# Memory keys and values computed under the second normalisation and kept in DRAM, two barriers taken out, and a gate product placed between the steps of the memory attention

## The reference, cut to what matters

```python
x = first_block(...)                          # ends with  h + y @ w_out   (w_out0, w_out1)
h = rmsnorm(x, g_mix)                         # "norm h2"
gq, gk, gv, gg, ga, dq, dk, dv, iq, ik, iw, mq, gates = split(h @ w_in)
o_gla = gla(gq, gk, gv, gg, ga)               # 4 linear-attention heads, state carried over 8 chunks
o_dsa = dsa(dq, dk, dv, iq, ik, iw)           # 8 heads; 128 keys chosen for each query by top-k
mem_h = rmsnorm(mem, g_mem)                   # 256 memory rows of 1024: does not depend on x
k, v = split(mem_h @ w_mem_kv)                # [256, 2048]; keys normalised for each of 4 heads
o_mem = softmax(norm(mq) @ norm(k).T) @ v     # 4 heads of 256
merged = sum(sigmoid(gates[b] + bias[b]) * (o_b @ w_o_b) for b in (gla, dsa, mem))
x = x + merged @ w_out                        # then 16 experts, 2 for each token
```

## Time and profile before

| | us |
|---|---|
| median of 3 runs (1584.70 to 1585.95) | 1585.25 |
| profiled execution, its own time | 1584.4 |
| its span, first to last instruction | 1582.5 |
| PE busy | 1393.1 (88% of the span) |
| DVE / ACT / POOL busy | 582.9 / 532.2 / 415.4 |
| mean granted TensorE clock | 0.923 of full |

### The profile page before, as it was taken

How to read it: one execution, slowest core, us unless ns; L and a number is a source line. 1 busy time by engine, 2 the same in 40 slices (tenths; PEclk the granted TensorE clock), 3 DMA queues, 4 the chain that set the end, 5 groups by cost and what they waited for, 6 DMA issues and landing times. The chain is left out here.

```text
span 1582.5 us, 16443 instructions
## 1 busy us (share of the span) xinstructions
PE 1393.1 (88%) x6220; PEld 1030.6 (65%) x6220; DVE 582.9 (37%) x1322; ACT 532.2 (34%) x945; POOL 415.4 (26%) x201
## 2 busy tenths in 40 slices
PE   4999979997789998999888976999799998699992
PEld 3777756675667766758667865877678876344440
DVE  2195554424221142349954433131341234221213
ACT  4442323213234463543335453244342224010100
POOL 3265211001233322215222213475205431000001
PEclk9999989857999999999989997999799998699996
DMA  4232423002222312113121213244105433799815
GB/s 139 61 92 67 154 67 101 22 2 70 80 67 66 95 33 74 54 53 107 60 65 49 61 53 99 94 142 125 45 17 197 173 120 147 305 358 366 298 67 187
DMA packets 75015, 175.35 MB, mean 111 GB/s; under 512 B 11166, under 2 KB 21588, under 8 KB 68788
## 3 DMA queue, kind: packets, MB, share of 16 engines
q1 hardware_dynamic: 67312, 161.28, 30.5%
q0 software_dynamic: 2592, 8.41, 1.5%
q10 hardware_dynamic: 5028, 4.55, 1.1%
HBM read 151.15 MB, written 23.07 MB: 110 GB/s over the span
## 5 line engine op out<-in xcount | busy, mean ns | idle before, releaser
L792 POOL TENSOR_TENSOR w_lo<-raw,w_hi 128x1024 fp32r<-128x1024 f32 (+1 forms) x158 | 377.6, 2407 | 884.4 <-ACT w_hi L1499 884.3
L887 PE MATMUL ps<-w_hi,act_hi 128*128 128x512 f32 (+1 forms) x560 | 236.0, 421 | 5.5 <-ACT dq L1659 4.0
L888 PE MATMUL ps<-w_lo,act_hi 128*128 128x512 f32 (+1 forms) x560 | 221.7, 396 | 0.0
L1499 ACT ACTIVATE w_hi<-raw 128x1024 fp32r<-128x1024 f32 (+1 forms) x158 | 158.7, 1033 | 186.5 <-PE ps L889 185.1
L889 PE MATMUL ps<-w_hi,act_lo 128*128 128x512 f32 (+1 forms) x560 | 220.9, 395 | 0.0
L887 PE MATMUL ps<-w_hi,mix_hi 128*128 128x512 f32 x320 | 134.1, 419 | 17.5 <-DVE gate L2157 9.9
L887 PEld LDWEIGHTS ps<-w_hi,act_hi 128*128 128x128 f32 (+1 forms) x560 | 106.1, 189 | 47.1 <-issue 15.2
L889 PE MATMUL ps<-w_hi,mix_lo 128*128 128x512 f32 x320 | 128.1, 400 | 0.0
L888 PE MATMUL ps<-w_lo,mix_hi 128*128 128x512 f32 x320 | 128.0, 400 | 0.0
L888 PEld LDWEIGHTS ps<-w_lo,act_hi 128*128 128x128 f32 (+1 forms) x560 | 106.1, 189 | 25.6 <-issue 3.3
L889 PEld LDWEIGHTS ps<-w_hi,act_lo 128*128 128x128 f32 (+1 forms) x560 | 105.6, 189 | 25.6
(11 more groups left out here) (419 smaller groups left out, 2027.1 us busy)
## 6 DMA issues: line engine op xcount, KB each, us to landing
raw<-in_w_in SPq DMA_DIRECT2D x92, 512.0 KB, 3.6
gu<-in_w_gate SPq DMA_DIRECT2D x16, 1024.0 KB, 6.5
gu<-in_w_up SPq DMA_DIRECT2D x16, 1024.0 KB, 8.7
dn<-in_w_down SPq DMA_DIRECT2D x16, 1024.0 KB, 9.9
x_rows<-zeros SPq DMA_DIRECT2D x16, 512.0 KB, 4.9
raw<-in_w_out SPq DMA_DIRECT2D x16, 512.0 KB, 4.0
raw<-in_w_mem_kv SPq DMA_DIRECT2D x16, 512.0 KB, 3.9
xe<-x_rows SPq DMA_DIRECT2D x16, 512.0 KB, 9.3
```

Source lines behind the costliest of these rows:

```text
L792: pool.tensor_tensor(lo[:, 0:a], raw[:, g % RAW_SLOTS, 0:a], hi[:, 0:a].bitcast(F32), ALU.subtract).then_inc(*POOL.done(("w_lo", g)))
L887: pe.matmul(dst, l_hi, r_hi, start=start, stop=False, skip_group_check=skip)
L888: pe.matmul(dst, l_hi, r_lo, start=False, stop=False, skip_group_check=skip)
L1499: nc.scalar.activation(split_slot(g)[0][:, 0:a], raw[:, g % RAW_SLOTS, 0:a], ACTF.Copy).then_inc(*ACT.done(("w_hi", g)))
```

## The change

The memory norm and its products move to the end of the first block and around `norm("h2")`; keys and values are written to two DRAM tensors and read back before the memory attention; the barriers `mem` and `mem2` go; `w_o00` joins the list that the top rounds are spread over; 12 parts of `gate20` and four query transposes go between the memory attention steps; three takes no longer stand ahead of the first block's attention; the turn of linear heads 1 and 3 moves ahead of the values of the head before.

```diff
@@ mla_order
     fill += [tail[0:2], tail[2:4]]
-    order, fill = sum(fill[0:3], []), fill[3:]
-    order += [("mla_transposes", 0), ("mla_transposes", 1)]
+    order = [("mla_transposes", 0), ("mla_transposes", 1)]
...
-    return order
+    last = item("w_out1")
+    return order + [("norm_scale", "mem")] + last[0:8] + [("norm", "mem")] + last[8:]
@@ make_order
-    order += mla_order() + item("w_out1") + [("barrier", "gla")]
-    order += [("norm", "h2")] + item("small2", "gla_q", "gla_k")
+    order += mla_order() + item("mem_kv0") + [("barrier", "gla"), ("norm_scale", "h2")] + item("mem_kv1") + [("mem_scale", "k")]
+    order += item("mem_kv2") + [("norm", "h2"), ("mem_prepare", "k")] + item("mem_kv3")
+    order += item("small2", "gla_q", "gla_k")
...
-    for h in range(GLA_H):
-        order += [("gla_states", h), ("gla_values", h)]
-        if h == 1:
-            order += [("gla_decays", 2)] + g0[0:8] + [("gla_decays", 3), ("gla_rstd", 0)] + g0[8:]
+    order += [("gla_turn", 0), ("gla_update", 0), ("gla_turn", 1), ("gla_values", 0), ("gla_update", 1), ("gla_values", 1)]
+    order += [("gla_decays", 2)] + g0[0:8] + [("gla_decays", 3), ("gla_rstd", 0)] + g0[8:]
+    order += [("gla_turn", 2), ("gla_update", 2), ("gla_turn", 3), ("gla_values", 2), ("gla_update", 3), ("gla_values", 3)]
...
-    dense += [("dsa_prepare", "q0"), ("dsa_scale", "q1")] + item("gate00") + [("dsa_prepare", "q1")]
-    order += spread(dense, rounds) + item("w_o00")
+    dense += [("dsa_prepare", "q0"), ("dsa_scale", "q1")] + item("gate00") + [("dsa_prepare", "q1")] + item("w_o00")
+    order += spread(dense, rounds)
...
-    order += [("mix_dsa",), ("barrier", "mem"), ("norm_scale", "mem"), ("norm", "mem")]
-    order += item("w_o10", "gate11", "w_o11", "mem_kv0", "mem_kv1") + [("mem_scale", "k")]
-    order += item("mem_kv2", "mem_kv3", "mem_q0")
-    order += [("mem_prepare", "k"), ("mem_scale", "q0")] + item("mem_q1") + [("mem_prepare", "q0"), ("mem_scale", "q1")]
-    order += [("mem_prepare", "q1"), ("barrier", "mem2")]
+    order += [("mix_dsa",)] + item("w_o10", "gate11", "w_o11", "mem_q0") + [("mem_scale", "q0")]
+    order += item("mem_q1") + [("mem_prepare", "q0"), ("mem_scale", "q1")]
     n = NT * MEM_H
+    steps = []
     for j in range(n + 3):
-        order += [("mem_values", j - 3)] * (j >= 3) + [("mem_turn", j - 2)] * (2 <= j < n + 2) + [("mem_scores", j)] * (j < n)
-    order += item("gate20", "w_o20", "gate21", "w_o21")
+        steps += [[("mem_values", j - 3)] * (j >= 3) + [("mem_turn", j - 2)] * (2 <= j < n + 2) + [("mem_scores", j)] * (j < n)
+                  + [("mem_turn_q", j + 2)] * (2 <= j < 6)]
+    g2 = item("gate20")
+    order += [x for s in spread(steps, [[p] for p in g2 if p[3] < 3]) for x in s] + [p for p in g2 if p[3] == 3]
+    order += [("route_start",)] + item("w_o20", "gate21", "w_o21")
@@ program
-        MEM_BANKS = (7, 3, 1, 2, 7, 3, 1, 2)
+        MEM_BANKS = (7, 3) * 4
+        def split_upto(name, u, b):
+            if name == "gate20":
+                ends = {0: min(u + 3, KC // 2), NT - 1: u + 4}
+            else:
+                ends = {0: u + 3}
+            return min(len(units), first_unit[name] + ends[b]) if b in ends else None
@@ sync
+                    if names[g] == ("gla_v0", 0):
+                        sp.wait_ge(*ACT.after("mkT", KC - 1))
+                        sp.dma_start(mem_keys, mkT_new[:, :, :].rearrange("p c n -> p (c n)")).then_inc(mem_spilled, 16)
+                        sp.wait_ge(*ACT.after("mkv", 3, 1))
+                        sp.dma_start(mem_vals, mv_new[:, :, :].rearrange("p c n -> p (c n)")).then_inc(mem_spilled, 16)
+                    if names[g] == ("mem_q0", 0):
+                        sp.wait_ge(mem_spilled, 32)
+                        sp.wait_ge(*PE.after("d_O", NT * DSA_H - 1))
+                        sp.wait_ge(*DVE.after("mix_lo", "dsa", DSA_H - 1))
+                        sp.dma_start(mkT[:, :, :].rearrange("p c n -> p (c n)"), mem_keys).then_inc(mem_back, 16)
+                        sp.dma_start(mv[:, :, :].rearrange("p c n -> p (c n)"), mem_vals).then_inc(mem_back, 16)
@@ scalar, norm_scale
                 if name == "mem":
+                    for h in (MLA_H - 2, MLA_H - 1):
+                        act.wait_ge(*PE.after("qT", "mla", h))
+                        act.wait_ge(*PE.after("kT", "mla", h))
+                    for t in range(2):
+                        act.dma_start(mem_in[:, t, :], w["mem_2"][0, P * t:P * t + P, :]).then_inc(mem_landed, 16)
                     act.wait_ge(mem_landed, 32)
@@ tensor, new step; scores
+            def mem_turn_q(c):
+                claim(6, (ACT, ("mqT", c)))
+                for t in range(NT):
+                    pe.wait_ge(*DVE.after("mqn", 1, t))
+                    tr = pe.transpose(ps[:, 6, P * t:P * t + P], mq[:, t, P * c:P * c + P], ident[:, :])
+                tr.then_inc(*PE.done(("mqT", c)))
             def mem_scores(j):
+                if j == 0:
+                    pe.wait_ge(mem_back, 32)
+                pe.wait_ge(*ACT.after("mqT", 2 * h + 1))
@@ scalar and vector: the seven routing DMAs of barrier mem2 and DVE's r_start are now the step route_start
+            def route_start():
+                act.wait_ge(*PE.after("m_O", NT * MEM_H - 1))
...
@@ ACT's gla_values(0) and DVE's gla_update(0)
+                if h == 0:
+                    act.wait_ge(mem_spilled, 32)
```

More of the change, by code:

```diff
@@ L307, in program @@
     x_rows = nc.dram_tensor("x_rows", (N_EXP * E_ROWS, D), F32, kind="Internal").ap()
+    mem_keys = nc.dram_tensor("mem_keys", (P, 8 * MEM), F32, kind="Internal").ap()
+    mem_vals = nc.dram_tensor("mem_vals", (P, 2 * D), F32, kind="Internal").ap()
     y_rows = nc.dram_tensor("y_rows", (N_EXP * E_ROWS, D), F32, kind="Internal").ap()
@@ L437, in program @@
         m_sq = sb("m_sq", [P, 2, 512], 97)
[L438 to L441, removed]
+        mem_in = sb("mem_in", [P, 2, D], SC)
+        mem_sc = sb("mem_sc", [P, 2, D], SC + 12)
+        mk = sb("mk", [P, 2, D], SC)
+        mv_new = sb("mv_new", [P, 2, D], SC + 37)
+        mkT_new = sb("mkT_new", [P, 8, MEM], SC + 45)
+        mv = sb("mv", [P, 2, D], SC + 62.5)
         mkT = sb("mkT", [P, 8, MEM], SC + 33.5)
-        mem_hi = sb("mem_hi", [P, KC, MEM], SC + 41.5, F32R)
-        mem_lo = sb("mem_lo", [P, KC, MEM], SC + 49.5, F32R)
+        mem_hi = sb("mem_hi", [P, KC, MEM], SC + 20, F32R)
+        mem_lo = sb("mem_lo", [P, KC, MEM], SC + 28, F32R)
         mqT = sb("mqT", [P, 8, SEQ], SC + 41.5)
@@ L861, in _ @@
                     POOL.section = a[0]
-                    if a[0] == "mem2":
-                        pool.memset(all_ones[:, :], float(N_EXP)).then_inc(*POOL.done(("all_ones",)))
+                elif step == "route_start":
+                    pool.wait_ge(*PE.after("m_O", NT * MEM_H - 1))
+                    pool.memset(all_ones[:, :], float(N_EXP)).then_inc(*POOL.done(("all_ones",)))
                 elif step == "small":
                     split_low(min(len(units), first_unit[a[0]] + 3))
-                elif step == "part" and a[2] == 0:
-                    split_low(min(len(units), first_unit[a[0]] + a[1] + 3))
+                elif step == "part" and split_upto(*a):
+                    split_low(split_upto(*a))
                 elif step == "pos":
@@ L1126, in gla_states, with gla_update @@
                 mm.then_inc(*PE.done(("g_att", h)))
+            def gla_update(h):
+                s = h % 2
                 pe.wait_ge(*ACT.after("g_keT", h))
@@ L1256, in mem_turn @@
                 for b in range(2):
-                    tr = pe.transpose(ps[:, 6, P * b:P * b + P], m_prob[:, j % 3, P * b:P * b + P], ident[:, :])
+                    at = P * b
+                    tr = pe.transpose(ps[:, 6, at:at + P], m_prob[:, j % 3, P * b:P * b + P], ident[:, :])
                 tr.then_inc(*PE.done(("m_PT", j)))
@@ L1440, in _ @@
                     gla_decays(*a)
-                elif step == "gla_states":
-                    gla_states(*a)
+                elif step == "gla_turn":
+                    gla_turn(*a)
+                elif step == "gla_update":
+                    gla_update(*a)
                 elif step == "gla_values":
@@ L1462, in _ @@
                     mem_scores(*a)
+                elif step == "mem_turn_q":
+                    mem_turn_q(*a)
                 elif step == "mem_turn":
@@ L1673, in evict @@
                         nc.scalar.activation(m_sq[:, b, :], ps[:, b, :], ACTF.Square).then_inc(*ACT.done(("mk_sq", 2 * n + b)))
-                    if (n, b) == (0, 0):
-                        act.wait_ge(*DVE.after("merged", 1, 1, NT - 1))
-                    dst = (mk if n < 2 else mv)[:, b, 512 * (n % 2):512 * (n % 2) + 512]
+                    dst = (mk if n < 2 else mv_new)[:, b, 512 * (n % 2):512 * (n % 2) + 512]
                     nc.scalar.activation(dst, ps[:, b, :], ACTF.Copy).then_inc(*ACT.done(("mkv", n, b)))
```

(12 more changed lines are left out.)

37 lines of the change are left out of this document (19 added, 18 removed).

## The result

The median of four runs is 1535.6 us (1529.9 to 1540.5) against 1585.0 of the kernel before in the same comparison: ratio 0.9688, 95% interval [0.9647, 0.9729], 49.3 us faster, where 31.7 were forecast and the range ended at 1541. The profiled execution took 1532.1, its span 1530.0, 52.5 less than before. In a second comparison the changed kernel took 1536.8 (five runs, 1531.0 to 1539.2) against 1583.2, ratio 0.9704 [0.9683, 0.9726].

The account below looks back on a forecast made before the run. PE, busy 88% of the span, was taken as the bound, through its waits and clock. Terms 12.3 + 8.8 + 10.8 - 0.8 + 0.6 = 31.7 off 1584.4 gave 1552.7, median 1553.6; range 1541 to 1569.

Parts of the forecast that it names:

- Step 4: First block's attention: 3.3 us more idle at the start, 3.9 gained in the last steps, 0.6 gained; bounds -5 and +6.
- Step 1: Memory norm and products moved: the load of the memory rows and the norm behind it go, 12.3 us gained.
- stop in `mem_kv1`: PE idle 4.0 us in `mem_kv1`, its third unit's split queued behind ACT's four squares.
- the 3.0 added for the half level: Memory work: 3.0 us for the half level behind the 4.0 stop and the broken transposes, 91.5 to 94.5.
- Step 2: `w_o00` under the top rounds: fewer rounds ahead of the eviction of `gate00`, 8.8 us gained; bounds 4 to 13.7.
- the 5.7 of idle for `gate_sum`: PE there at 782, eviction of `gate00` ending at 787.7 by a walk of DVE's queue: 5.7 us idle.
- the 1.7 for the clock: From `dsa_q0` to the end of `w_o00`: 1.7 us added for the clock, 813.0 to 814.7.
- Step 3: Memory attention: shorter chain to the first turn and `gate20` parts between the steps, 10.8 us gained; bounds 5 and 14.
- Bought back: First expert's load ahead of `w_o20`'s second unit lands late behind the memory attention: 0.8 us lost; bounds 0 and 4.
- At nothing: Priced at no change: turns of heads 1 and 3, the 2 MB written and 2 MB read, `route_start`.
- B: Better cover: neither the 4.0 stop nor the clock losses appear, `w_o00` under the top rounds gains 13.7; 1541 us; chance 0.12.
- D: Interleaved memory attention and transposes around both norms run at the half level; slower than before, 1601 at 60 us; chance 0.05.

Follow-up runs that it names:

- the two experiments: Three takes ahead of the first block's attention dropped in the kernel before: 1576.5 against 1583.2 us; put back in the changed kernel: 1545.0 against 1536.8.
- places 18 and 22: Changed kernel with retention heads beginning at place 18 (three takes put back, 8.2 us slower) or 22 (one empty place ahead, 14.0 slower), instead of 21.
- both experiments: `w_o00` alone put under the top rounds in the kernel before: 1573.8 against 1583.4 us; taken out again in the changed kernel: 1546.5 against 1536.8.
- the experiment: Changed kernel with the parts of `gate20` behind the memory attention's steps instead of between them: 1536.0 us, ratio 0.9704 to the kernel before.

## Why the prediction was wrong

The direction and three of four mechanisms held; the size failed, by 17.6 us (49.3 against 31.7), and the largest part of it in one step.

**Step 4 is the step that failed (0.6 forecast; 11.6 in the first profile, 6.7 and 8.2 by the two experiments).** The term left out is PE's busy time, which changes with the clock; it was put at nothing without a reason. The two experiments make 6 to 8 of the missing 17.6; that the first profile shows 11.6 is in part luck, since it is of an execution under the median (1532.1 against 1535.6). I summed idle: 3.3 lost at the start, 3.9 gained at the tail. The loss came (k_sb 5.3, at 171.55, 3.6 expected), and idle as a whole fell by 2.0, so the bookkeeping of idle was good. The bounds were the fault: they were worked out from idle too, -5 to +6, while the earlier trace rows showed a stretch at clock 0.76 right there. In the runs the same 1037 instructions keep PE busy for 193 to 217 us, by where the fill falls between the attention's steps and, at one and the same order, from execution to execution (193.5 and 199.7). I had a row of the clock and priced only the waits beside it. That the place of the fill does it is shown for places 18 and 22 against 21; whether the heads or the `w_out0` takes carry it, and why place 21 is better than 22, stays open.

**Step 1 (12.3; 13.6).** Each wait came as forecast: transposes 3.1 for 3.0, barrier 1.6 for 1.6, stop in `mem_kv1` 3.8 for 4.0, the transposes around the norm 8.3 for 8.8, 1.8 for 1.7 in `w_o10`. The sum was 91.5, and 94.5 with the half level; 92.6 were measured. About half of the 3.0 added for the half level is there: right behind the stop 3.4 us run at it, which costs some 1.5. And 22.4 us in the earlier trace rows hold 99 products, not 96; the 96 of `w_out1` take 21.9 (405.96 to 427.88), so each item was set a little too long.

```profile
440.80:444.20 3.40, 3.40 (x10) 2.66 (x9) 3.40 (x2) 0.00 (x0) 3.40 (x2) 0.50 0.55 177
```

By the Trainium skill's rule (SBUF — State Buffer, "SBUF: two separate sides") the gain would have been some 2 less. The trace agrees on the engines: while the second key scaling runs, two of POOL's subtractions take 3.1 and 3.4 us instead of 2.4. PE's share is less than the 2: it waits 0.9 for them (0.58 and 0.29). Duration in ns, shortest, median and longest:

```profile
L817 POOL TENSOR_TENSOR w_lo<-raw,w_hi x3: 2392/3085/3382, 450.3 to 456.7; 128x1024 fp32r<-128x1024 f32 x3
L2369 DVE TENSOR_TENSOR mk<-mk,ss x2: 1224/2320/3415, 449.9 to 451.1; 128x1024 f32<-128x1024 f32 x2
```

**Step 2 (8.8; 9.7 by both experiments).** The mis-sized term is the 5.7 of idle for `gate_sum`: it was 1.3 and 0.3. The count was right (33 rounds ahead of it, nine fewer), the walk of DVE's queue was not. Nine rounds at 1.51 are 13.6, and 797.2 - 13.6 is 783.6 for the end of the eviction; it ended at 813.0, which is 782.7 with `dsa_q0` set at the same time. My walk from 718 ended at 787.7.

```profile
812.34 0.68 DVE L2210 TENSOR_TENSOR gate<-ps,gate_bias 128x512 f32<-128x512 f32 x1
```

PE's arrival at 782 was 1.4 earlier than 787.4 less the 4.0 gives, and yet it came at 781.5. The wait for POOL was 1.8 for 2.1, and the 1.7 for the clock didn't come (the stage is at 1.00). Against this stand 4.8 us in the sparse attention that I had not put down: idle 7.5 instead of 5.6, clock 0.96 instead of 0.99. A part of the gain is lost again there.

**Step 3 (10.8; 13.7).** Chain 8.7 for 9.0, last parts 5.7 for 5.6, bank 3 0.6 for 0.9. The middle took 52.9 where 55.8 were forecast: in the profile of the experiment the interleaving saves 5.8 in these stretches, where my terms come to 1 to 3; the times show no difference. Bought back: no wait for the raw load (0.8 forecast) but 0.9 in `gate21` for the eviction of `w_o20` (L2221).

**At nothing:** g_keT still 7.1; the spills and `route_start` show no wait of PE.

**Rivals.** B came nearest (1541), only in part for its own reasons: the clock's share behind the two stops is small, as it had it, but the 3.8 of the stop is there and step 2 came to 9.7, not 13.7. The largest part, step 4, is not in it. D is out, the two new stages run at 0.98 and 0.97. The rule of the Trainium skill that D came to (TensorE: Matmul & The Clock Gate, "Part 1: The HAM clock gate") has the engine's activity set the level; the trace of the kernel with the heads one place later has PE busy 86.4 of 88.7 us and the clock at the half level throughout, so busy time as the profile counts it doesn't tell the level.

## What to carry to other kernels

Where a stretch's clock is under 1, its price belongs into the sum and above all into the bounds, even if the edit changes no wait there: here a shift by one place of 37 moved the time by 14 us at equal idle (22.2 in both stretches). Try neighbouring placements of such a stretch rather than argue for one, and take more than one profile of a kernel before a difference of a few us in it is given a cause. For what DVE evicts late, subtract the removed instructions from the measured time instead of walking the queue anew.

## What the runs showed of the hardware that was not expected

- PE at work almost without a pause for 72 to 101 us (96% to 98% busy) had a mean clock between 0.58 and 0.87, so at 0.58 most of the stretch was at the 1.2 GHz level: 88.7 us on end, with PE busy for 86.4 of them. The share changes between executions of one kernel (0.72 and 0.81).
- Products that write the lower and the upper 64 partitions of one bank in turn overlap: 96 in 9.3 us, against 19.0 when one of the pair takes all 128 and the two no longer alternate. This agrees with the Trainium skill (TensorEngine Tiling (Array Packing), "Key Properties"), by which tiles of the array work independently.
- Three vector scalings of 128x1024 that run beside POOL's subtractions take 2.85 to 2.87 us each, the one ahead of them 0.75 (`xs`, 436.9 to 446.0 in the changed kernel).
- Runs of the kernel before, which lay within 2.5 us of each other in the first comparison (four runs), lie between 1572.7 and 1587.6 in the later ones.
